# Another order for the last MLP group and the final norm of a streaming encoder step

## The reference, cut to what matters

```python
def sq_relu_mlp(hn, w_up, w_down):
    return jnp.square(jax.nn.relu(hn @ w_up)) @ w_down      # 1024 -> 4096 -> 1024
...
hp = hp + sq_relu_mlp(rmsnorm(hp, g_mlp[l]), w_up[l], w_down[l])     # prompt; the sample's hs likewise
...
y_prompt = rmsnorm(hp, g_final)      # x * rsqrt(mean(x*x) + EPS) * g
y_sample = rmsnorm(hs, g_final)
```

## Time and profile before

| | us |
|---|---|
| median of 3 runs | 1806.37 (1803.94 to 1808.28) |
| the profiled execution's own time | 1806.5 |
| its span, first to last instruction | 1804.7 |
| last matmul begins | 1780.51 |
| last `final_scale` begins | 1796.14 |
| last DMA is issued | 1797.46 |

### The profile page before, as it was taken

One profiled execution on the slowest core, in us unless ns is written; L12 is line 12 of the kernel. 1 busy time (PEld: TensorE's weight loads), 2 busy tenths in 40 slices (PEclk: granted clock), 3 DMA queues, 4 the chain that ended last, 5 costly groups with the idle time before them and its releaser, 6 DMA issues.

```text
span 1804.7 us, 30795 instructions
## 1 busy us (share of the span) xinstructions
PE 1704.0 (94%) x11713; PEld 1569.0 (87%) x11713; DVE 1084.6 (60%) x1930; ACT 738.4 (41%) x1471; POOL 446.1 (25%) x547
## 2 busy tenths in 40 slices
PE   6998989997898999999999999999999999999993
PEld 5997889886788999988799999999999999999982
DVE  5556656765556435224422777777777777777775
ACT  5123335476555113025511544444444444444443
POOL 2113322112122101100000133333333333333336
PEclk9999999999999999999999999999999999999997
DMA  6312322245565505336351111111111111111102
GB/s 217 109 65 62 88 87 85 68 158 181 181 217 189 184 24 215 124 128 229 111 210 37 34 48 34 37 46 46 46 46 46 46 46 46 46 46 32 37 12 105
DMA packets 107530, 170.37 MB, mean 94 GB/s; under 512 B 7544, under 2 KB 75768, under 8 KB 107416
## 3 DMA queue, kind: packets, MB, share of 16 engines
q1 hardware_dynamic: 79512, 126.78, 20.8%
q0 software_dynamic: 8160, 22.29, 3.6%
q10 hardware_dynamic: 19760, 19.92, 3.5%
HBM read 138.17 MB, written 31.72 MB: 94 GB/s over the span
## 4 chain that ended last, share of the span: by engine, by line
PE 85%; DVE 5%; ACT 3%; issue 3%; DMA 2%; POOL 2%; SPq 0%; DVEq 0%; ACTq 0%; POOLq 0%
PE banks L2184 24%; PE banks L2607 22%; PE banks L2617 19%; PE banks L2230 6%; PE banks L2385 2%; PE banks L2328 2%; PE banks L2507 1%; PE banks L2172 1%; PE banks L2415 1%; PE banks L2487 1%; PE banks L2455 1%; PE banks L2476 1%; DMA w_raw<-in_cache_mem_k 1%; ACT probs L1332 1%; POOL h L1110 1%
## 5 line engine op out<-in xcount | busy, mean ns | idle before, releaser
L1110 POOL TENSOR_TENSOR h<-h,added 128x512 f32<-128x512 f32 x192 | 262.6, 1375 | 500.1 <-ACT added L1137 485.2
L2184 PE MATMUL banks<-w_hi,xt_hi 128*128 128x256 f32 x1224 | 355.4, 290 | 16.3 <-DVE stage L1658 4.3
L2184 PE MATMUL banks<-w_hi,xt_lo 128*128 128x256 f32 x1224 | 344.5, 281 | 0.0
L2184 PE MATMUL banks<-w_lo,xt_hi 128*128 128x256 f32 x1224 | 344.4, 281 | 0.0
L2607 PE MATMUL banks<-xt_hi,w_hi 128*128 128x384 f32 x768 | 258.4, 336 | 0.0
L2607 PE MATMUL banks<-xt_hi,w_lo 128*128 128x384 f32 x768 | 258.1, 336 | 0.0
L2607 PE MATMUL banks<-xt_lo,w_hi 128*128 128x384 f32 x768 | 258.1, 336 | 0.0
L2184 PEld LDWEIGHTS banks<-w_hi,xt_hi 128*128 128x128 f32 x1224 | 233.2, 191 | 25.3 <-issue 8.5
L2078 DVE TENSOR_TENSOR h<-h,banks 128x512 f32<-128x512 f32 x304 | 206.2, 687 | 75.6 <-PE banks L2617 73.5
L2184 PEld LDWEIGHTS banks<-w_lo,xt_hi 128*128 128x128 f32 x1224 | 233.3, 191 | 0.0
L2184 PEld LDWEIGHTS banks<-w_hi,xt_lo 128*128 128x128 f32 x1224 | 232.9, 190 | 0.0
(11 more groups left out here) (271 smaller groups left out, 3364.0 us busy)
## 6 DMA issues: line engine op xcount, KB each, us to landing
w_raw<-in_w_up SPq DMA_DIRECT2D x16, 1024.0 KB, 5.4
w_raw<-in_w_down SPq DMA_DIRECT2D x16, 1024.0 KB, 4.8
w_raw<-in_w_xkv ACTq DMA_DIRECT2D x8, 1024.0 KB, 6.3
kc_diff<-in_cache_diff_k SPq DMA_DIRECT2D x16, 512.0 KB, 5.6
vc_diff<-in_cache_diff_v SPq DMA_DIRECT2D x8, 1024.0 KB, 5.5
w_raw<-in_cache_mem_k SPq DMA_DIRECT2D x16, 512.0 KB, 7.4
w_raw<-in_w_in ACTq DMA_DIRECT2D x7, 1024.0 KB, 5.4
scaled<-mix_d SPq DMA_DIRECT2D x9, 512.0 KB, 4.9
```

The source lines that it names most:

```text
L1110: pool.tensor_tensor(dst, dst, added[:, n % 2, :], ALU.add).then_inc(s_padd, 1)
L2184: last = mm(out, xt[:, k, tok:tok + P], w[:, k, :], start=(k == 0 and n == 0), stop=(k == KD - 1 and n == 2))
```

## The change

- **PE.** In the last group the sample's products move from among phase 1's to between the two phases, and use banks 3 and 2 in place of 3 and 4 (`pairs(end, 1, ...)` gets no single part).
- **ACT.** In the last group the first two `product_out` come before `squared(end, 2)`; `single_hi` comes before `batch_hi`; `final_square(0)` comes after `product_out(5)`; `product_out` 8 to 11 are gone. The squares are taken in the order 0, 8, 1, 2, 3, ... Three tiles, 8, 1 and 2, are multiplied by rstd on ACT (`final_by_act`).
- **DVE.** The first four additions come before `batch_mixed`, the next four before `single_lo` and `batch_lo`; the sample's three additions follow the lows. Phase 1's last four products for the left half are added by DVE from PSUM (`add_last`). `final_scale` is left for tiles 0 and 3 to 7.
- **POOL.** Four of the twelve additions are gone. It multiplies tiles 8, 1 and 2, scaled by ACT, by the gain (`final_gain`, 128 x 1024), the last of them behind all nine `rsqrt`.
- **SP.** The tiles leave in the order 0, 8, 3, 1, 4, 5, 2, 6, 7.

```diff
@@ SP
-            for t in range(TT):
-                sp.wait_ge(s_y, t + 1)
+            for n, t in enumerate((0, 8, 3, 1, 4, 5, 2, 6, 7)):
+                if t in BY_POOL:
+                    sp.wait_ge(s_yp, BY_POOL.index(t) + 1)
+                else:
+                    sp.wait_ge(s_y, (0, 3, 4, 5, 6, 7).index(t) + 1)
@@ POOL
-            add_phase(NG - 1, 0)
-            for t in range(4):
-                rsqrt(F_FIN + t)
-            add_phase(NG - 1, 1)
-            for t in range(4, TT):
-                rsqrt(F_FIN + t)
+            def final_gain(t):
+                pool.wait_ge(s_ys, BY_POOL.index(t) + 1)
+                pool.wait_ge(s_gain, 16 * 4)
+                pool.tensor_tensor(h[:, t, :], h[:, t, :], gain_final, ALU.mult).then_inc(s_yp, 1)
+            end = NG - 1
+            add_phase(end, 0)
+            rsqrt(F_FIN)
+            for n, tile in ((6, 4), (7, 6)):
+                pool.wait_ge(s_padd, end * U_ACT + n)
+                add_copied(end, n, tile)
+            rsqrt(F_FIN + 1)
+            rsqrt(F_FIN + 2)
+            final_gain(8)
+            rsqrt(F_FIN + 3)
+            final_gain(1)
+            rsqrt(F_FIN + 4)
...
+            rsqrt(F_FIN + 8)
+            final_gain(2)
@@ ACT
+            def final_by_act(t):
+                n = final_no(t)
+                act.wait_ge(s_rstd, n + 1)
+                copy(h[:, t, :], h[:, t, :], scale=rstd[:, n:n + 1]).then_inc(s_ys, 1)
...
             relu(end, 2)
-            squared(end, 2)
             product_out(end, 0)
             product_out(end, 1)
+            squared(end, 2)
+            act.wait_ge(s_square, end * 3 + 3)
+            single_hi(end)
             batch_hi(end, True)
-            single_hi(end)
-            for n in range(2, 8):
+            for n in range(2, 6):
                 product_out(end, n)
-            for t in range(4):
+            final_square(0)
+            product_out(end, 6)
+            product_out(end, 7)
+            for t in FINAL_ORDER[1:4]:
                 final_square(t)
-            for n in range(8, 12):
-                product_out(end, n)
-            for t in range(4, TT):
+            for n, t in enumerate(BY_POOL):
+                final_by_act(t)
+                final_square(n + 3)
+            for t in (6, 7):
                 final_square(t)
@@ DVE
+            def add_last(g):
+                for n, (t, bank) in enumerate(((4, 6), (5, 4), (6, 7), (7, 5))):
+                    dst = h[:, t, 0:512]
+                    dve.wait_ge(s_pa, g * U_ACT + (9 + n))
+                    dve.wait_ge(s_padd, g * U_ACT + 8)
+                    V.tensor_tensor(dst, dst, ps[bank], ALU.add).then_inc(s_hlast, 1)
...
+            add_some(end, 0, 0, 4)
             batch_mixed(end)
-            add_some(end, 0, 0, 4)
+            add_some(end, 0, 4, 8)
+            single_lo(end, True)
             batch_lo(end, True)
-            single_lo(end)
-            add_some(end, 0, 4, 8)
-            add_some(end, 1, 0, 4)
+            add_single_last(end)
             final_scale(0)
-            add_some(end, 1, 4, 8)
-            add_single(end)
-            for t in range(1, TT):
+            add_some(end, 1, 0, 8, 11)
+            add_last(end)
+            for t in (3, 4, 5, 6, 7):
                 final_scale(t)
@@ PE
-            pairs(NG - 1, 0, HID, False)
-            pairs(NG - 1, 1, HID_END, True)
+            end = NG - 1
+            pairs(end, 0, HID, False, 0, 4)
+            pe.wait_ge(s_hlo, end * U_HID + 5)
+            pe.wait_ge(s_relu, end * 3 + 2)
+            product(3, 0, "b11", None, True, SINGLE, s_pv)
+            product(2, 1, "b21", None, True, SINGLE, s_pv)
+            pe.wait_ge(s_hadd, end * U_VEC + 9)
+            product(3, 0, "t1", None, False, SINGLE, None)
+            product(3, 1, "b22", None, False, SINGLE, s_pv)
+            pairs(end, 1, HID_END, False, 11, 7)
```

More of the change, by code:

```diff
@@ L444, in build @@
         s_padd = sem("s_padd")
+        s_hlast = sem("s_hlast")
         s_y = sem("s_y")
+        s_ys = sem("s_ys")
+        s_yp = sem("s_yp")
         s_yd = [sem("s_yd0"), sem("s_yd1")]
@@ L466, in norm_no, with final_no @@
             return f if f < F_MIX else f - TT
+        def final_no(t):
+            return norm_no(F_FIN + FINAL_ORDER.index(t))
         def mem_no(m):
@@ L1122, in _ @@
                 add_phase(i, 1)
-            add_phase(NG - 1, 0)
-            for t in range(4):
-                rsqrt(F_FIN + t)
-            add_phase(NG - 1, 1)
-            for t in range(4, TT):
-                rsqrt(F_FIN + t)
+            def final_gain(t):
[14 more added lines that the diff above has]
+            rsqrt(F_FIN + 4)
+            rsqrt(F_FIN + 5)
+            rsqrt(F_FIN + 6)
+            rsqrt(F_FIN + 7)
+            rsqrt(F_FIN + 8)
+            final_gain(2)
             pool.wait_ge(s_cache, 32)
@@ L1502, in final_square @@
             def final_square(t):
-                vec = (5, 6, 7, 8, 13, 14, 15, 16, 19)[t]
+                vec = (5, 6, 7, 8, 16, 17, 18, 19, 11)[t]
                 act.wait_ge(s_hadd, (NG - 1) * U_VEC + vec)
[L1506 to L1509, removed]
+                if t < 4:
+                    act.wait_ge(s_padd, (NG - 1) * U_ACT + (3, 4, 5, 6)[t])
+                elif t < PT:
+                    act.wait_ge(s_hlast, t - 3)
+                n = final_no(t)
+                if n >= norm_no(F_FIN) + 2:
                     act.wait_ge(s_sq, n - 1)
-                nc.scalar.activation(square_out[:, t % 2, :], h[:, t, :], ACT.Square,
+                nc.scalar.activation(square_out[:, n % 2, :], h[:, t, :], ACT.Square,
                                      accum_out=sumsq[:, n:n + 1]).then_inc(s_sq, 1)
+            def final_by_act(t):
+                n = final_no(t)
+                act.wait_ge(s_rstd, n + 1)
+                copy(h[:, t, :], h[:, t, :], scale=rstd[:, n:n + 1]).then_inc(s_ys, 1)
             def hidden_ahead(g):
@@ L2063, in batch_lo, with single_lo @@
                 hi, lo, hs, ls = (end_hi, end_lo, end_s_hi, end_s_lo) if last else (hid_hi, hid_lo, hs_hi, hs_lo)
-                dve.wait_ge(s_hhi, g * U_HID + 5)
+                dve.wait_ge(s_hhi, g * U_HID + (5 + last))
                 V.tensor_tensor(lo, sq[:, :, 4 * P:8 * P], hi.bitcast(F32), ALU.subtract).then_inc(s_hlo, 1)
-                dve.wait_ge(s_hhi, g * U_HID + 6)
+                dve.wait_ge(s_hhi, g * U_HID + (6 + last))
                 V.tensor_tensor(ls, s_tmp, hs.bitcast(F32), ALU.subtract).then_inc(s_hlo, 1)
-            def single_lo(g):
-                dve.wait_ge(s_hhi, g * U_HID + 7)
+            def single_lo(g, last=False):
+                dve.wait_ge(s_hhi, g * U_HID + (5 if last else 7))
                 V.tensor_tensor(h8_lo, sq[:, :, SEQ:TOK], h8_hi.bitcast(F32), ALU.subtract).then_inc(s_hlo, 1)
@@ L2078, in add_product, with add_some @@
                 V.tensor_tensor(dst, dst, ps[bank], ALU.add).then_inc(s_hadd, 1)
-            def add_some(g, phase, first, end):
+            def add_some(g, phase, first, end, base=8):
                 t = 4 * phase
@@ L2084, in add_some @@
                     if n >= 4:
-                        dve.wait_ge(s_hadd, g * U_VEC + (8 * phase + (2, 1, 4, 3)[n - 4]))
-                    add_product(g, 8 * phase + n, t + (1, 0, 3, 2, 0, 1, 2, 3)[n], 1, (6, 4, 7, 5, 6, 4, 7, 5)[n])
+                        dve.wait_ge(s_hadd, g * U_VEC + (base * phase + (2, 1, 4, 3)[n - 4]))
+                    add_product(g, base * phase + n, t + (1, 0, 3, 2, 0, 1, 2, 3)[n], 1, (6, 4, 7, 5, 6, 4, 7, 5)[n])
             def add_single(g):
@@ L2619, in product, with pairs @@
                     last.then_inc(done, 1)
-            def pairs(g, phase, hid, single):
+            def pairs(g, phase, hid, single, d, lows):
                 vec, act_ = g * U_VEC, g * U_ACT
-                d, c = 8 * phase, 6 * phase
-                pe.wait_ge(s_hlo, g * U_HID + (4 + 2 * phase))
+                c = 6 * phase
+                pe.wait_ge(s_hlo, g * U_HID + lows)
                 if phase == 0:
```

15 lines of the change are left out of this document (11 added, 4 removed).

## The result

The changed kernel takes 1803.98 us in the median of 12 runs (1801.60 to 1809.67), the kernel before, run beside it, 1808.02 (1803.94 to 1809.72, 12 runs). The ratio is 0.9981, with a 95% interval of 0.9973 to 0.9990: 3.4 us faster (1.8 to 4.9; the two medians alone differ by 4.0), at the edge of what I had called no change (0.2%). The forecast was 1806.0, the range 1802.8 to 1808.4. The time lies in the range, but the gain that I forecast, 0.5 us, lies outside the interval.

A forecast was written before the change was run, and what follows sets the result against it. PE's matrix work is 85% of the chain; only the 52.5 us after the last `up` can shrink. POOL's last multiplication ends at 1794.3, the last DMA lands at 1799.6, plus 4.6 gives span 1804.2, time 1806.0; range 1802.8 to 1808.4.

The forecast's parts named there:

- the case that DVE has the first turn: DVE's lows alternate with POOL's phase 0 additions: they end at 1765.9 if DVE goes first, 1766.85 if POOL does.
- PE's new wait: Before the sample's third product, PE waits 2.6 to 3.5 us for DVE's addition standing behind the slowed lows.
- Turns on two SBUF inputs: DVE and POOL instructions that each read two SBUF tiles cannot run together; they alternate, one of each.
- Rival A: DVE's lows run unslowed beside POOL's additions, ending at 1763.4; time 1803.6, 2.4 us below the forecast; chance 0.17.
- rival C: POOL's three multiplications cost more, slower from 3.9 us each; at 4.3 us each the time is 1811.4; chance 0.06.
- The remaining 4.6 us hold no work: At the span's end, after the last DMA lands at 1800.1, nothing runs until 1804.7.
- With the same 4.6 us behind it the span is 1804.2: The last DMA lands at 1799.6 instead of 1800.1, and the 4.6 us piece behind it stays equal.
- DVE's last `final_scale` starts first, so POOL is blocked until 1791.8 and ends at 1794.3: At the end, POOL's multiplication of tile 2 waits for DVE's last scaling, then takes 2.5 us.
- rival B: POOL's last multiplication hides beside `final_scale`, so DVE's end counts, 1791.85 against 1797.43; time 1800.9; chance 0.09.

The follow-up runs named there:

- e5: Changed kernel plus three POOL fills that nobody waits for behind its last multiplication; tail (last `up` to span's end) 51.3 us against 49.1, one run.
- e7: Changed kernel plus one small POOL instruction ahead of tile 2's multiplication, giving DVE the first turn; tail 49.8 us against 49.1, one run.
- e8: Changed kernel plus three unread filler products in PE's wait ahead of the sample's third product; tail 48.4 us against 49.1, one run.
- e2: Changed kernel without its third part: POOL makes all nine `rsqrt`, DVE scales all nine tiles; tail 43.9 us, ratio 0.9944 against the kernel before.
- e6: Kernel where DVE scales all tiles (e2), with one pair of POOL instructions making rstd of tiles 4 to 7; tail 40.4 us, ratio 0.9942.
- e10: Kernel before with one edit: one pair of POOL instructions makes rstd of tiles 4 to 8; tail 47.7 us against 52.5, ratio 0.9969.

## Why the prediction was right in the time and wrong in its last step

**What held.** Times less 2.1 for the other start. The last matmul began at 1780.87, 1778.7 by before's count (forecast 1778.4). The lows ended at 1765.6 (1765.9 for the case that DVE has the first turn). PE's new wait was 2.46 (2.6 to 3.5). POOL's additions ended at 1773.6 (1773.5). The multiplications took 2.34 to 2.42 (2.5). The rstd of tile 3 was there at 1782.4 (1782.5), that of tile 7 at 1790.4 (1790.5), rounds of 2.0 us between them, DVE idle for 2.5 (3). Three transfers left close together and moved data for 4.0 us (3.9). Turns on two SBUF inputs are confirmed: 2.33 for 1.21, 2.01 for 0.94, and 7.01 for four additions. The Trainium skill (GPSIMD Engine Reference, section 3.1) had led to an estimate of 2.25 for the multiplication, so the runs lie between the two. Rival A, lows at their free length, fell by the 2.33 and 2.01, and rival C by 2.42, far below its 3.9.

**What of this was luck.** The prediction has no drop of PE's clock, and this execution had one. In e5, e7 and e8, with the same order and no drop, the last matmul began at 1777.2 by before's count, 1.2 ahead of the forecast, and POOL's first two multiplications and the rstds behind them came 0.7 to 0.8 earlier. The agreement to 0.1 us from 1773.5 on is two errors that cancel: the stretch ahead of it was faster than forecast, and the drop gave that back. The time was helped too: the kernel before measured 1808.0 beside the changed one and not the 1806.4 that I had started from, and 1806.4 x 0.9981 would be 1802.9, at the lower edge of the range. (1806.0 is 0.4 under that 1806.4, not the 0.1 that the prediction says.)

**The step that failed: "The remaining 4.6 us hold no work", and with it "With the same 4.6 us behind it the span is 1804.2".** The piece behind the landing is no constant. Those 4.6 us were the end of POOL's DRAIN, which runs to 8.35 us behind POOL's last instruction. The span ends 8.6 us behind that instruction, as eleven of twelve kernels show to within 0.07 us, e5 by lengthening POOL's work alone. In the kernel before, POOL's last instruction is this row of its timeline:

```profile
1795.56 0.55 POOL L1013 TENSOR_TENSOR rstd<-rstd,mhalf 128x1 f32<-128x1 f32 x1
```

It ends at 1796.11, 1.3 us ahead of DVE; the chain closed with DVE's last scaling and its DMA, and I followed it there. In neither of the two kernels did the end wait for the last landing (1800.1 in both executions). What the change did to the time is what it did to POOL's end: 43.9 to 40.5 us from the end of `up`, 3.4 us, and the tail is shorter by the same 3.4. With my own forecast for POOL's end, 1794.3, the rule gives a span of 1802.9 and a gain of 1.8 in place of 0.5.

**The term that was mis-sized: "DVE's last `final_scale` starts first, so POOL is blocked until 1791.8 and ends at 1794.3".** It ended at 1792.7, 1.6 us earlier. A `rsqrt`'s first instruction starts 0.08 us behind the one ahead of it, DVE 0.04 behind, so DVE has the turn; but the multiplication, a `tensor_tensor` that follows a `tensor_tensor` and does not wait for it, starts 0.03 before that one ends. The trace of before had this case already, where phase 1's additions follow a `rsqrt` that ends at 1776.68:

```profile
1776.65 9.68 POOL L1110 TENSOR_TENSOR h<-h,added 128x512 f32<-128x512 f32 x6
```

e7 makes the order I assumed, and POOL ends 1.4 later. DVE pays: its last scaling ended at 1793.8 by before's count, 1.9 behind the forecast, and closes the chain in place of POOL's multiplication. 1.8 and 1.6 make the 3.4. The prediction had priced the unblocked case under rival B (1793.0), but only to set it aside.

**Rival B** (DVE's end counts, 1800.9) forecast a gain of 5.6, 2.2 above the measured 3.4 where mine was 2.9 below it, and had the cause wrong: DVE's end moved 3.7 us, but e7 shows that DVE can end 2 us earlier and the tail get longer.

**Where the expected gain went.** The two first parts are worth 8.6 us of the tail. The third gives 5.2 back (e2 against the changed kernel, both with the drop): `final_gain` costs 2.4 us of the same turns for which `final_scale` needs 1.29, delays each rstd behind it, and, being POOL's last instruction, moves the end.

**Open.** The profile shows that POOL's DRAIN takes the 8.35 us, but not what it waits for in them (DVE's DRAIN in the kernel before ends 0.1 us behind DVE's last instruction), and no run separated it. Why the clock fell behind the same wait in four executions and not in three is open too; nor was it tried whether DVE can make the rstds, so that POOL is out of the end altogether.

## What to carry to other kernels

Follow each engine to its last instruction and on to what its queue does at the program's end, and not the last DMA alone: in this program the end came 8.6 us behind the last POOL instruction, so whatever POOL does last must come early. Work shared between DVE and POOL is only shared if the two don't take turns; three POOL multiplications of 2.4 us in place of three of DVE of 1.29 lost 5.2 us. Small POOL instructions that alternate with long DVE ones cost up to a whole DVE instruction each, so make one of them for several tiles (2 to 3.5 us in e6, 4.8 in e10).

## What the runs showed of the hardware that I had not expected

- A DRAIN of POOL's queue at the program's end finished 8.35 us behind POOL's last instruction in all twelve kernels. The end of the span stood 8.56 to 8.63 us behind that instruction in eleven, and 9.66 in the one whose last DMA came late, 0.4 us behind that DMA's landing.
- A POOL `tensor_tensor` behind another one for which it does not wait began 0.03 us before that ended; one that waits for the one ahead (the additions within a phase), or a `tensor_scalar`, began 0.08 us behind it. Where both engines were ready, this went with who had the next turn (3.35 or 1.28 us for the same DVE instruction).
- With the same PE wait of about 2.4 us the granted clock fell to 0.50 for some 3 us in four executions, at the wait's end or 0.9 to 1.0 us behind it, and not at all in three; a drop cost PE 1.5 us and the end 0.6 to 0.8.
- `scalar_tensor_tensor` with two SBUF tiles takes turns with POOL's `tensor_scalar` of one element per partition as it does with a large addition (1.29 for 0.19).
